# A hybrid decoder layer in float32: seven block products instead of eight in part of the feed-forward matrix products

## The reference

```python
def swiglu(h, w_gate, w_up, w_down):
    return (jax.nn.silu(h @ w_gate) * (h @ w_up)) @ w_down

h = rmsnorm(x, norm_mix_g[l]);  x = x + hybrid_mixer(h, ...)
h = rmsnorm(x, norm_xq_g[l]);   x = x + memory_cross_attention(h, mem_n, ...)
h = rmsnorm(x, norm_ffn_g[l]);  x = x + swiglu(h, w_ffn_gate[l], w_ffn_up[l], w_ffn_down[l])
return rmsnorm(x, norm_final_g)
```

## Time and profile before

| | us |
|---|---|
| median of 3 runs | 1782.18 (1781.26 to 1783.38) |
| the profiled execution, its time | 1781.97 |
| its span, first to last instruction | 1779.5 |
| TensorE (PE) busy | 1765.7 (99%) |
| VectorE (DVE) busy | 997.1 (56%) |
| ScalarE (ACT) busy | 898.8 (51%) |
| mean DMA rate | 190 GB/s |

### The profile page before, as it was taken

The page is one execution under the profiler, slowest core; times in us unless marked ns, Lnnn a source line. Parts: engine busy times, 40 slices in busy tenths (PEclk is TensorE's granted clock), DMA queues, the critical chain, the costliest instruction groups (busy, mean ns, idle before and its releaser), DMA issues.

```text
span 1779.5 us, 20521 instructions
## 1 busy us (share of the span) xinstructions
PE 1765.7 (99%) x8052; PEld 1469.1 (83%) x8052; DVE 997.1 (56%) x1020; ACT 898.8 (51%) x1111; POOL 27.0 (2%) x51
## 2 busy tenths in 40 slices
PE   8999999999999999999999999999999999999998
PEld 7888888888888888888888888888888888888886
DVE  6577677655455554555665565555554445555554
ACT  6767668444545554544555464444443344444443
POOL 1000000000000000000000000000000000000000
PEclk9999999999999999999999999999999999999999
DMA  8565665666565756566755466666666666666654
GB/s 278 172 200 167 196 202 187 203 197 170 176 212 162 216 159 190 171 191 211 245 183 187 144 179 189 190 189 190 189 188 195 192 196 190 190 189 189 188 192 142
DMA packets 175740, 337.99 MB, mean 190 GB/s; under 512 B 10672, under 2 KB 15280, under 8 KB 175152
## 3 DMA queue, kind: packets, MB, share of 16 engines
q1 hardware_dynamic: 173232, 327.72, 60.9%
q0 software_dynamic: 1008, 5.24, 0.9%
q10 hardware_dynamic: 1424, 3.97, 0.6%
HBM read 334.80 MB, written 2.10 MB: 189 GB/s over the span
## 4 chain that ended last, share of the span: by engine, by line
PE 99%; DMA 0%; issue 0%; ACT 0%; DVE 0%; ACTq 0%; POOLq 0%; POOL 0%; DVEq 0%
PE group L383 31%; PE group L385 31%; PE group L384 31%; PE side L395 2%; PE side L496 0%; PE side L480 0%; DMA x_T_in<-in_x_T 0%; PE group L620 0%; PE group L618 0%; PE group L619 0%; PE side L451 0%; PE side L450 0%; PE side L449 0%; PE side L559 0%; PE side L478 0%
## 5 line engine op out<-in xcount | busy, mean ns | idle before, releaser
L972 DVE TENSOR_TENSOR w_lo<-w_raw,w_hi 128x1024 fp32r<-128x1024 f32 x612 | 747.6, 1224 | 713.1 <-ACT w_hi L646 711.8
L646 ACT ACTIVATE w_hi<-w_raw 128x1024 fp32r<-128x1024 f32 x612 | 647.0, 1060 | 809.2 <-PE group L385 785.0
L383 PE MATMUL group<-w_hi,x_hi 128*128 128x512 f32 x1628 | 638.2, 392 | 2.0 <-DVE w_lo L1020 2.0
L385 PE MATMUL group<-w_hi,x_lo 128*128 128x512 f32 x1628 | 634.4, 390 | 0.0
L384 PE MATMUL group<-w_lo,x_hi 128*128 128x512 f32 x1628 | 634.3, 390 | 0.0
L383 PEld LDWEIGHTS group<-w_hi,x_hi 128*128 128x128 f32 x1628 | 306.1, 188 | 64.5 <-issue 2.4
L385 PEld LDWEIGHTS group<-w_hi,x_lo 128*128 128x128 f32 x1628 | 306.1, 188 | 63.9
L384 PEld LDWEIGHTS group<-w_lo,x_hi 128*128 128x128 f32 x1628 | 306.1, 188 | 62.2
L383 PE MATMUL group<-w_hi,v_hi 128*128 128x512 f32 x320 | 125.2, 391 | 0.0
L385 PE MATMUL group<-w_hi,v_lo 128*128 128x512 f32 x320 | 124.6, 389 | 0.0
L384 PE MATMUL group<-w_lo,v_hi 128*128 128x512 f32 x320 | 124.5, 389 | 0.0
(11 more groups left out here) (245 smaller groups left out, 1058.5 us busy)
## 6 DMA issues: line engine op xcount, KB each, us to landing
w_raw<-in_w_in SPq DMA_DIRECT2D x223, 512.0 KB, 3.9
w_raw<-in_w_ffn_gate SPq DMA_DIRECT2D x88, 512.0 KB, 3.9
w_raw<-in_w_ffn_up SPq DMA_DIRECT2D x88, 512.0 KB, 3.7
w_raw<-in_w_ffn_down SPq DMA_DIRECT2D x88, 512.0 KB, 4.6
w_raw<-in_w_rnn_proj SPq DMA_DIRECT2D x32, 512.0 KB, 4.6
w_raw<-in_w_attn_proj SPq DMA_DIRECT2D x32, 512.0 KB, 4.3
w_raw<-in_w_mix_out SPq DMA_DIRECT2D x32, 512.0 KB, 4.2
w_raw<-in_w_xkv SPq DMA_DIRECT2D x16, 512.0 KB, 3.5
```

The costliest lines, as they stand in the source:

```text
L383: nc.tensor.matmul(gps[p][:, tt, :], xh[:, kt, tok], whi[:, s, k, :], start=kt == 0, stop=False)
L385: last = nc.tensor.matmul(gps[p][:, tt, :], xl[:, kt, tok], whi[:, s, k, :], start=False, stop=end)
L646: nc.scalar.activation(whi[:, s], raw[:, s], ACT.Copy).then_inc(hi_ready[s], 1)
L972: V_.tensor_tensor(wlo[:, s], raw[:, s], whi[:, s].bitcast(F32), ALU.subtract).then_inc(w_ready[s], 1)
```

## The change

In the feed-forward part two groups are now worked on together: gate and up of one inner group, or two neighbouring down groups. The sequence of chunks alternates between the two. A plan lists the pairs of row tiles: `O` is as before, two chunks of 12 matmuls, one of each group. `W` takes the 2 x 2 blocks (two token tiles x two row tiles, times two row tiles x two groups) by Strassen's scheme in Winograd's form, seven block products instead of eight, 21 matmuls instead of 24. A `W` fills four slots: A and B are loaded as before, C and D hold sums of A and B that DVE makes in `raw` (`weight_sums`), and all four are split into high and low parts (of B the second tile alone). Its matmuls are 6, 3, 6 and 6. Four of the products accumulate in the four banks of `side` (P1, Q5, P7, P6) and three straight in the groups' buffers. After the last `W` of a pair ACT and DVE combine the four banks into `fold`, and `join` adds the groups' buffers to it. Sums of the activations are made once (`x2_sums`, `inner_sums`) and split too.

Gate and up: pair 0 of part a has no `W`, the other ten pairs have two each. Down: both pairs of part a have four each, the first pair of part b three; the last two groups of b are as before. The hardware loops are written out. Silu is now made in the next pair, from `fold` (`gate_tanh`, `inner_tok`), and the scaled copy L928 is gone. Some semaphores of the first half of the program were merged, with the same instructions.

```diff
+UP_PLAN = "O0 O1 O2 W3 O4 W5 O6 O7".split()
+DOWN_PLAN = {"a": "O0 O1 O3 W2 O5 W4 O7 W6 O9 W8 O10 O11".split(),
+             "b": "O0 O1 O3 W2 O5 W4 O7 W6 O8 O9".split()}
...
+        steps += [("O", kp, 0), ("O", kp, 1)] if step[0] == "O" else [("A", kp, 0), ("B", kp, 1), ("C", kp, None), ("D", kp, None)]
...
+        P1, Q5, P7, P6 = [side[i // 2][:, 2 * (i % 2):2 * (i % 2) + 2, :].rearrange("p a b -> p (a b)") for i in range(4)]
...
+            def pair(first, ws, row0, cols):
+                for c, (_, kp, half) in enumerate(STEPS[first]):
+                    if half is not None:
+                        load(N0[first] + c, ws[half], row0 + kp * CK * P, cols[half])
...
+                    if kind == "A":
+                        products(P1, xh[:, k0, tok0], xl[:, k0, tok0], s, 0, begin, end)
+                        last = products(gps[p0][:, 0, :], xh[:, k1, tok0], xl[:, k1, tok0], s, 1, False, False)
+                    if kind == "B":
+                        last = products(gps[p1][:, 0, :], sh[:, w, 3, :], sl[:, w, 3, :], s, 1, False, False)
+                    if kind == "C":
+                        products(Q5, sh[:, w, 0, :], sl[:, w, 0, :], s, 0, begin, end)
+                        last = products(gps[p0][:, 1, :], xh[:, k1, tok1], xl[:, k1, tok1], s, 1, False, False)
+                    if kind == "D":
+                        products(P7, sh[:, w, 2, :], sl[:, w, 2, :], s, 0, begin, end)
+                        last = products(P6, sh[:, w, 1, :], sl[:, w, 1, :], s, 1, begin, end)
+                    last.then_inc(w_used[s], 1)
...
+                        if KIND.get(m) == "A":
+                            weight_sums(m)
+                        ks = slice(1, 2) if KIND.get(m) == "B" else slice(0, CK)
                         dve.wait_ge(hi_ready[s], used + 1)
-                        V_.tensor_tensor(wlo[:, s], raw[:, s], whi[:, s].bitcast(F32), ALU.subtract).then_inc(w_ready[s], 1)
+                        V_.tensor_tensor(wlo[:, s, ks], raw[:, s, ks], whi[:, s, ks].bitcast(F32), ALU.subtract).then_inc(w_ready[s], 1)
+            def weight_sums(m):
+                for half in range(2):
+                    s, used = slot_of(m + half)
+                    dve.wait_ge(raw_full[s], 16 * (used + 1))
+                a, (c, used), (d, _) = 2 * (m % R), slot_of(m + 2), slot_of(m + 3)
+                for s in (c, d):
+                    dve.wait_ge(w_ready[s], START + used)
+                T1_T3 = tiles[:, 2 * c:2 * c + 3:2, :]
+                then(V_.tensor_tensor(T1_T3, tiles[:, a:a + 4:3, :], tiles[:, a + 2:a + 3, :].to_broadcast([P, 2, GW]), ALU.add))
+                then(V_.tensor_tensor(raw[:, d, 1], raw[:, c, 0], tiles[:, a + 3, :], ALU.add))
+                dve.sem_inc(raw_full[d], 16)
+                V_.tensor_tensor(raw[:, c, 1], raw[:, d, 1], tiles[:, a + 1, :], ALU.add).then_inc(raw_full[c], 16)
...
+                if at_ is not None and c == at_ + 1:
...
+                    then(V_.tensor_tensor(fold[:, 1, 0, :], fold[:, 0, 0, :], P6, ALU.subtract))
+                    then(V_.tensor_tensor(fold[:, 0, 1, :], fold[:, 1, 0, :], P7, ALU.subtract))
+                if at_ is not None and c == at_ + 2:
+                    V_.tensor_tensor(fold[:, 1, 1, :], Q5, fold[:, 0, 1, :], ALU.subtract)
+                    then(V_.tensor_tensor(fold[:, 1, 0, :], Q5, fold[:, 1, 0, :], ALU.subtract))
...
+                    V_.tensor_tensor(fold[:, half], fold[:, half], gps[p][:, :, :], ALU.add).then_inc(taken[p], 1)
```

More of the change, by code:

```diff
@@ L381, in gemm @@
                             tok = slice(tt * P, (tt + 1) * P)
[L382 to L385, removed]
+                            last = products(gps[p][:, tt, :], xh[:, kt, tok], xl[:, kt, tok], s, k, kt == 0, kt == tiles - 1)
@@ L566, in _, with inner_T @@
                         res_T("x2", GI["cross_out", j - 1], j - 1)
-            def inner_T():
+            def inner_T(i):
+                pe.wait_ge(sem("inner_tok"), i)
                 transpose(stage[0], side[0], "inner_T")
+            folds, sums_made, inners = 0, min(1, len(X_SUMS)), 0
+            pe.wait_ge(sem("x2_lo"), 2)
             for part, groups in (("a", FA), ("b", FB)):
[L572 to L604, removed]
@@ new lines, in _, with gate_tanh, inner_split @@
+            made = [0, 0, 0]
+            def gate_tanh(first):
+                wait_taken(act, GI[first])
+                for tt in range(TT):
+                    last = nc.scalar.activation(silu[:, tt, :], fold[:, 0, tt, :], ACT.Tanh, scale=hrstd["x2"][:, tt:tt + 1])
+                last.then_inc(sem("tanh"), 1)
+            def inner_split(kt0, summed):
+                made[0] += 1
+                act.wait_ge(sem("inner_T"), made[0])
+                if summed:
+                    nc.scalar.activation(f_in[:, :, :], side[0][:, 0:CK, :], ACT.Copy)
+                nc.scalar.activation(inner_hi[:, kt0:kt0 + NB, :], side[0][:, :, :], ACT.Copy).then_inc(sem("inner_hi"), 1)
@@ new lines, in sums_lo, with inner_tok @@
+            def sums_lo(dst, src, hi):
+                made[2] += 1
+                dve.wait_ge(sem("sums_hi"), made[2])
+                V_.tensor_tensor(dst, src, hi.bitcast(F32), ALU.subtract).then_inc(sem("sums_lo"), 1)
+            def inner_tok(first):
+                made[0] += 1
+                dve.wait_ge(sem("tanh"), made[0])
+                then(V_.scalar_tensor_tensor(silu[:, :, :], silu[:, :, :], 1.0, fold[:, 0], ALU.add, ALU.mult))
+                for tt in range(TT):
+                    last = V_.scalar_tensor_tensor(stage[0][:, tt, :], fold[:, 1, tt, :], silu_scale[:, tt:tt + 1], silu[:, tt, :], ALU.mult, ALU.mult)
+                last.then_inc(sem("inner_tok"), 1)
```

434 lines of the change are left out of this document (289 added, 145 removed).

## The result

| | before | after |
|---|---|---|
| median | 1782.29 us (4 runs, 1781.26 to 1783.38) | 1835.50 us (3 runs, 1831.70 to 1838.41) |
| ratio, 95% interval | | 1.0297, 1.0272 to 1.0321 |
| profiled execution, its span | 1779.5 us | 1829.5 us |

The change is slower by 3%, and the prediction of 1792 (range 1771 to 1807) was wrong: right in its sign, far too small in size. The two spans differ by 50.0 us.

The account below looks back on a forecast made before the run. PE, busy 99% of the span, was taken as the bound. Stalls were to outweigh the 21.1 us saved: net +4 us in gate and up, +6.5 in down, about +10 on 1781.97, giving 1792 us (range 1771 to 1807).

Parts of the forecast that it names:

- The bound and the saving: Feed-forward part: PE is the bound; 31 `W` at 0.68 us each save 21.1 us if everything else hides.
- Rival 5: In a `W`: the seventh product is not saved, as PE runs shorter matmul pieces slower; given no chance of its own.
- The chain from E: From PE's start of a pair's first `W`, through loads, sums and splits: stalls of 1.7 us gate and up, 2.3 down.
- each further W: 1.4: Down pairs, each `W` after the second: a round of 11.3 to 12.0 us against PE's 10.2, 1.4 us stall.
- Rival 2: Feed-forward loads: an idle queue lands them in 3.2 us, so the kernel gets faster, 1767 us; chance 0.19.
- Rival 1: Feed-forward loads: all landings at their short end, 3.5 to 3.8 us, so break-even at 1780 us; chance 0.20.
- Rival 3: Feed-forward loads: two loads 0.6 us apart share the engines, landing in 4.7 us and more, 1817 us; chance 0.12.
- two joins (2.4): DVE work over a pair: the two joins were counted as 2.4 us of its load.
- 38 us in PE's 43: DVE work over a whole pair: 38 us within PE's 43, so DVE is not full as a mean.
- Rival 4: Pairs: DVE's other work fails to hide, 0.3 us late in eleven pairs, 3 us on any case; no chance given.
- PE's busy time falls by about 21 us: Expected sign in the changed profile: PE's busy time falls by about 21 us, with new idle time before plain chunks.
- if PE's gaps stand between pairs, the timetable is wrong: Sign against the forecast: PE gaps at the transposes or between pairs would mean its timetable is wrong; no size given.

Follow-up runs that it names:

- one_each: The changed kernel in the order of `halves`, with one early `W` in each of the 13 pairs that had any, plain steps behind: 1771.72 us, ratio 0.9945.
- sum_twice: The changed kernel with the first weight sum (L1107) issued twice in every `W`: 1862.82 us, ratio 1.0456.
- pairs_plain: The changed kernel with every `W` replaced by plain steps, keeping the order by pairs and the late joins: 1798.59 us, ratio 1.0099.
- halves: The changed kernel with the first two and last two plain steps issued one group first, so the first buffer is joined two chunks earlier: 1813.50 us, ratio 1.0194.
- spread: `halves` with the `W` further apart, at least four plain chunks between two, 28 `W` in all: 1792.24 us, ratio 1.0068.

## Why the prediction was wrong

**The bound and the saving: right.** PE was the bound, and a `W` removes three matmuls worth 0.68 us: the instruction counts show the first, `one_each` the second. Rival 5, a seventh product that isn't saved, falls by it.

**The chain from E: right, and near in size.** 31 us of stalls were forecast, 34.7 were lost, each in front of the chunks named or of A just ahead of them. `sum_twice` shows that it is this chain. For gate and up 17 was forecast and 16.2 measured, with landings as assumed; for down 14 and 18.5. What was too low there was "each further W: 1.4": in the first down pair of part a, the second `W` lost 0.46 + 1.50 (forecast 2.3), the third 0.94 + 1.27, the fourth 0.89 + 2.33. The forecast took the round over the plain chunks to be the longer one, with a landing of 4.0 and up to 0.7 for a neighbour. It did not follow the load of B, which is issued behind three others and took 5.7 to 6.1 us: that round came last in all five, 12.6 to 13.0 us from sums to sums where 11.3 to 12.0 was forecast.

**Rivals 1 to 3, and the page's rule.** Rival 2 is refuted: no load on the chain landed in 3.2 us; the shortest took 3.5. The Trainium skill, "DMA: Bandwidth & Descriptors", section "Anatomy of one DMA — SWDGE (gpsimd) path", gives 3.2 us for 512 KB by its fit. That section is on DMAs that GpSimd issues, and these are issued by SP, so the fit is not tested here; it did not carry over to them: the loads of O6 went into an empty queue and took 3.9 us as a mean. Rival 1 was half right. In gate and up eight of the ten loads of B landed in 3.5 to 3.8 us, but those of O6 took 3.7 to 4.1, and the stalls stayed above the 1.36 us saved as a mean. Rival 3 (4.7 and more for both) came true nowhere in gate and up: where B took 4.7 and 4.8, O6 took 4.0 and 3.9.

**The step that failed: "two joins (2.4)".** They were counted as load on DVE, beside "38 us in PE's 43", and never as something that PE waits for. Rival 4 came near (a join holds back the next pair's splits), but it meant the splits and not the buffer, and put a late 0.3 us in eleven pairs on it, 3 us. The question that was not asked is who waits for the join: the next pair's first matmul, for the only buffer it can use. It cost 23.0 us: 12.7 in eleven gate and up pairs, 10.4 in three down pairs. `pairs_plain` shows it alone (17 us of span without any `W`), `halves` shows the 12.7 us of gate and up removed (18.7 us of span back, with what hangs on them).

**What a stall costs beyond its length: not priced.** The forecast said that stalls cost more than their length if the clock falls, and gave it no term. It was 6.2 us of half clock and single late matmuls, and 5.7 us of restarts.

**The smaller points.** The transposes, forecast to hide by a quarter of a us, do hide: no PE wait for `stage` is among the waits. "PE's busy time falls by about 21 us" was a bad test, since it fell by 1.9: busy times include the overlap of matmuls, which a wait ends, and the longer ones of the half clock. The count of matmuls and the distance of starts tell it. The forecast's "if PE's gaps stand between pairs, the timetable is wrong" is what happened.

As terms: forecast +10; joins +23.0, half clock and restarts +11.9, the chain +3.7 make 48.6, the measured sum up to rounding.

## What to carry to other kernels

When two accumulations are interleaved, ask of every buffer when it is emptied now and who stands waiting for it; work that was hidden behind the other buffer's turn comes to stand between two groups, and it costs that even if DVE is half idle. A step that takes all slots of a ring turns prefetching into a chain of load, work and load: add up that chain against the time to the next such step, and keep few enough of them, far enough apart (here one a pair, or six plain chunks between). A design that removes bound work should be tried first with the structure alone and nothing removed: here that price was 14.6 us of waits before anything was saved, and 23.0 with the `W`.

## What was not expected of the hardware

**Half clock behind short waits.** PE around a wait of 2.18 us in a down pair:

```profile
1380.72 0.57 PE L424 MATMUL group<-w_hi,inner_hi 128*128 128x512 f32 x1 [2.18 <-DVE w_lo L1094]
1381.09 0.63 PE L425 MATMUL group<-w_lo,inner_hi 128*128 128x512 f32 x1
1381.52 0.63 PE L426 MATMUL group<-w_hi,inner_lo 128*128 128x512 f32 x1
```
```profile
1381.00:1384.50 3.50, 3.50 (x10) 2.67 (x10) 2.19 (x2) 2.09 (x3) 0.00 (x0) 0.51 0.83 271
1470.00:1473.00 3.00, 3.00 (x8) 2.32 (x7) 1.57 (x2) 0.00 (x0) 0.00 (x0) 0.50 0.19 45
```

The same behind a wait of 1.83 us in `spread` (PE started again at 1310.90):

```profile
1312.00:1315.00 3.00, 3.00 (x8) 2.33 (x8) 3.00 (x3) 1.08 (x2) 0.00 (x0) 0.50 0.54 160
```

The granted clock is 0.51 and 0.50, the 1.2 GHz level, and matmuls start 0.43 us apart for about 3.5 us: some 8 of them, each 0.2 us late. In the changed kernel it followed the waits of 2.18 us here, of 3.71 us at 1469.36 and of 3.89 us at 1764.92, there for eleven matmuls; the wait of 2.27 us that ended at 1395.78 was followed by a clock of 1.00, and so were waits of 1.81 and 1.87 us in `spread` (1.00 from 1449 to 1452 and from 1583 to 1586). The length of the wait alone does not decide it; what else does was not tried.

**A restart has a price.** Behind each wait the second matmul starts 0.33 us after the first, not 0.227 (1255.24, 1255.57), and the next few 0.24 apart: about 0.14 us for each of 41 waits.

**Where a load stands among its neighbours went with its landing more than the mean load of the queue.** In the change C and D of a `W` load nothing, and the mean DMA rate fell from 190 to 185 GB/s. Yet the medians of gate, up and down are 4.2, 4.6 and 4.7 us against 3.9, 3.7 and 4.6. The loads now come in bunches. The 31 that were issued behind the split of an A, into an empty queue, took 3.7 to 4.9 us, as a median 3.9; the 13 loads of B issued 2.7 us behind A, or in one case 2.4, took 3.5 to 4.9, as a median 3.7; the five loads of B at the end of four within 2.9 us took 5.7 to 6.1. No run changes the spacing alone. Part of the rise may not be of the change: the loads of `w_in`, earlier in the program, went from 3.9 to 4.2 us as well.
